# A two-layer diffusion backbone on one core: when the modulation weights are read, how their rows are turned, and how three hand-overs are made

## The chip, the cores and the metric

The kernel runs on one core of a Trainium2 chip. Its time is the time of one execution on the device in microseconds, and lower is better. A core has five engines that run their own instruction streams and wait for one another by semaphores: TensorE (PE, with its weight loads PEld), VectorE (DVE), ScalarE (ACT), GpSimd (POOL) and SyncE (SP), which here issues the loads of weights.

## The reference

Two groups of tokens, 128 of context and 256 latent ones, pass through two layers that share one set of weights. A layer is a feed-forward (SwiGLU, 1024 to 2 x 2816 and back), a token mixer, and a second feed-forward. Each of the three is `x <- LN(ALPHA*x + gate*sublayer(x*(1+scale)+shift))`, with shift, scale and gate of every channel from a conditioning vector, one for context and one for latents:

```python
mod_ctx = einsum('d,lde->le', silu(c_ctx), w_mod) + b_mod      # 9 x 1024 values per layer
mod_lat = einsum('bd,lde->lbe', silu(c), w_mod) + b_mod
x = LN(ALPHA*x + 0.5*g1*swiglu(x*(1+sc1)+sh1))
x = LN(ALPHA*x + g2*mixer(x*(1+sc2)+sh2))
x = LN(ALPHA*x + 0.5*g3*swiglu(x*(1+sc3)+sh3))
```

The mixer runs three recurrences on one input projection, each in both directions: HGRN2 and mLSTM (four heads of 128) and a Mamba-2 scan (eight heads of 64, with a short convolution); their outputs are projected, merged by sigmoid gates and projected again. In mLSTM and Mamba each pair of head and direction needs `exp(row_t - row_s)` where s comes before t and 0 elsewhere, a masked 128 x 128 matrix per block of tokens. Everything is float32. Latent scans start from given states, and the final states of the context are outputs.

## The kernel before

All 384 tokens (three blocks of 128) go through together. Activations lie with channels on partitions, `x[:, c, :]` for the eight chunks of 128 channels. Weights are read once, as units of 128 x 1024 (512 KB), in the order of use. Four buffers hold units in turn. SyncE loads one (`raw`), ScalarE rounds it to float32r (`whi`, line 974), GpSimd subtracts (`wlo`, line 519, two halves of 512 columns), and TensorE multiplies `whi*h_hi + whi*h_lo + wlo*h_hi`, three one-pass products per chunk (lines 552 to 554, or 566 to 568 where three units are taken chunk by chunk). ScalarE's program rounds unit u+3 (`ahead`) where it comes to what follows unit u, after TensorE is done with unit u-1. Splits are told by `w_split`, finished units by `w_used`.

A modulation unit is another kind: its 1024 columns are the moving operand against the four columns of the conditioning vectors (`mod_product`, line 578: four products of 512 columns a unit). Four units make a group and give 4 x 512 numbers in one bank. ScalarE copies them to `modrow`, and TensorE turns them onto partitions by four small products with `pick` (`turn`, line 585; in the prologue line 925). VectorE adds the bias (`adaln`).

The order of work on TensorE is written out by hand:
1. Prologue: the 40 units (ten groups) of the first five modulations of layer 0, in a hardware loop with one group a turn of the loop, each group turned and only then the next one begun. VectorE takes 704 of the 1024 columns of each unit's remainder here, GpSimd 320. Behind them VectorE makes the modulated input, ScalarE rounds it (`high`), VectorE subtracts (`low`), and then ScalarE rounds the first three units of the feed-forward.
2. Feed-forward: 44 gate/up units in a loop of four, two per chunk of 128 hidden channels; ScalarE's tanh and four VectorE operations make `act_hi` and `act_lo`. Then all three engines meet (`ffn_met`: each drains, raises `met` and waits for the three), and 24 down units follow, three per output chunk. At layer 1's first feed-forward the meeting also clears the semaphores.
3. Layer norm: during the down units VectorE adds the residual, centres the chunk with an early mean, and sums chunks and squares (`sx`, `sqs`; `statistics`). Behind the last chunk TensorE multiplies the sums and the last chunk by a matrix of 1/1024; VectorE subtracts the mean (`shift`), takes the reciprocal of the root, scales, and writes `h_lo` of the next input while ScalarE writes the shifted and the rounded chunk.
4. Input projection (stage "in"): eight units `hf` and four `hq` go to banks 0 and 1 in turn (the first three to 0, 1, 2), then `hi` to 2, 3, 4 and `hg` to 5, 6, 7.
5. HGRN, mLSTM, Mamba, merging, output projection. The other projections and the modulation groups (`mod`, `turn`) stand at slots between the steps of the recurrences as filling work (`mixer_order`, `HG_FILL`): 18 groups in layer 0 (all nine modulations that come next), 8 in layer 1.

In mLSTM (eight rounds) and the pair products of Mamba (sixteen) a round begins with TensorE spreading a row over all partitions (`spread`, line 773: a float32 product with one column of `ident`, which the trace shows as two passes). VectorE adds the mask (`exps`, line 1808), ScalarE takes the exponential (`pair`), VectorE multiplies by the scores (`scores`), and TensorE goes on. VectorE's program does the addition of round r+1 before the scores of round r.

## Time and profile before

| what | value |
|---|---|
| median of 3 runs | 2798.45 us (2794.81 to 2804.83) |
| the profiled execution's own time | 2796.18 us |
| its span, first to last instruction | 2794.3 us |
| TensorE busy | 2431.0 us, 87% |
| GpSimd busy | 1518.8 us, 54% |
| VectorE busy | 1196.1 us, 43% |
| ScalarE busy | 1061.3 us, 38% |
| loaded from memory | 317.35 MB |

Shares are averages over stages of different kinds: a share below 100% of the engine with the most work is either a stop or products that the clock slowed. TensorE's clock is granted at 1.0 or at 0.5 of full speed, so a stretch between the two is a mean. A line such as 552 belongs to a helper and stands for all units of its kind; windows of time tell the stages apart.

### The profile page before, as it was taken

Reading aid. Unit: us, or ns where it says so; the run is one execution under the profiler, and the core shown is the slowest. Engines: PE = TensorE matmul, PEld = TensorE weight load, DVE = VectorE, ACT = ScalarE, POOL = GpSimd, SP = SyncE. Lnnn points to the kernel's source line nnn. Section 1 sums busy time; section 2 is a strip of 40 time slices with the busy share of each in tenths; the row PEclk is TensorE's granted clock in tenths of the full one; section 3 lists DMA queues with packets and bytes.
Section 4 is the critical chain, followed back from the end, with each engine's and each line's share of the span. In section 5 each row is a group of like instructions: output and inputs, shape, how many; then the busy total and the mean of one; then the engine's idle time right before and its main releaser. Section 6 shows DMA issues by size and latency. Waiting matters only on the chain. (4 is left out here: it accounts for less than half of the span.)

```text
span 2794.3 us, 38271 instructions
## 1 busy us (share of the span) xinstructions
PE 2431.0 (87%) x13246; PEld 2222.2 (80%) x13246; DVE 1196.1 (43%) x1923; ACT 1061.3 (38%) x1631; POOL 1518.8 (54%) x1164
## 2 busy tenths in 40 slices
PE   5599989898878887799998999889987787889997
PEld 2499989787646676699998999788775676889997
DVE  4543232562565326643225331526445543663314
ACT  4333235434444443343234322452444324143322
POOL 3376545565555774466664655456743432646653
PEclk8799999999989998999999999999998888899999
DMA  8443333344343552234343333333432221324432
GB/s 277 144 141 122 118 108 109 103 129 129 102 128 94 159 158 83 83 120 123 118 128 100 124 112 118 97 113 121 144 105 83 85 66 61 98 76 135 128 111 70
DMA packets 93459, 323.16 MB, mean 116 GB/s; under 512 B 11040, under 2 KB 14368, under 8 KB 92960
## 3 DMA queue, kind: packets, MB, share of 16 engines
q1 hardware_dynamic: 87552, 312.03, 35.8%
q10 hardware_dynamic: 5792, 9.56, 1.0%
q8 instruction: 76, 1.25, 0.2%
q14 instruction: 39, 0.32, 0.0%
HBM read 317.35 MB, written 4.20 MB: 115 GB/s over the span
## 5 line engine op out<-in xcount | busy, mean ns | idle before, releaser
L519 POOL TENSOR_TENSOR wlo<-raw,whi 128x512 fp32r<-128x512 f32 (+2 forms) x1160 | 1518.6, 1335 | 1243.2 <-ACT whi L974 1182.0
L974 ACT CAST whi<-raw 128x1024 fp32r<-128x1024 f32 (+1 forms) x600 | 615.8, 1036 | 998.8 <-PE ps L554 666.4
L552 PE MATMUL ps<-h_hi,whi 128*128 128x384 f32 x2224 | 762.9, 343 | 35.2 <-DVE h_lo L2025 13.0
L554 PE MATMUL ps<-h_hi,wlo 128*128 128x384 f32 x2224 | 752.8, 339 | 0.0
L553 PE MATMUL ps<-h_lo,whi 128*128 128x384 f32 x2224 | 752.7, 338 | 0.0
L552 PEld LDWEIGHTS ps<-h_hi,whi 128*128 128x128 f32 x2224 | 425.5, 191 | 45.6 <-DVE h_lo L2025 13.6
L553 PEld LDWEIGHTS ps<-h_lo,whi 128*128 128x128 f32 x2224 | 425.4, 191 | 2.6 <-issue 2.0
L554 PEld LDWEIGHTS ps<-h_hi,wlo 128*128 128x128 f32 x2224 | 424.6, 191 | 0.0
L552 PE MATMUL ps<-act_hi,whi 128*128 128x384 f32 x704 | 241.9, 344 | 11.5 <-DVEq L458 5.9
L553 PE MATMUL ps<-act_lo,whi 128*128 128x384 f32 x704 | 240.4, 341 | 0.0
L554 PE MATMUL ps<-act_hi,wlo 128*128 128x384 f32 x704 | 240.3, 341 | 0.0
L1479 DVE SCALAR_TENSOR_TENSOR x<-ps,mod,x 128x128 f32<-128x128 f32 x96 | 35.6, 412 | 349.5 <-PE ps L554 349.5
L1560 DVE SCALAR_TENSOR_TENSOR sb<-tb,ps 128x384 f32<-128x384 f32 x88 | 48.8, 554 | 245.2 <-ACT tb L1061 245.2
L578 PE MATMUL ps<-whi,cond_s 128*4 128x512 f32 x288 | 123.7, 430 | 34.5 <-POOL wlo L519 34.5
L552 PEld LDWEIGHTS ps<-act_hi,whi 128*128 128x128 f32 x704 | 133.7, 190 | 13.3 <-DVEq L458 6.9
L1569 DVE TENSOR_TENSOR act_lo<-vb,act_hi 128x384 f32 x88 | 131.2, 1490 | 10.8
L553 PEld LDWEIGHTS ps<-act_lo,whi 128*128 128x128 f32 x704 | 133.5, 190 | 0.5
L554 PEld LDWEIGHTS ps<-act_hi,wlo 128*128 128x128 f32 x704 | 133.6, 190 | 0.0
L1563 DVE SCALAR_TENSOR_TENSOR vb<-sb,ps 128x384 f32<-128x384 f32 x88 | 48.8, 554 | 180.2 <-PE ps L554 180.0
L578 PE MATMUL ps<-wlo,cond_s 128*4 128x512 f32 x288 | 121.2, 421 | 0.0
L686 PE MATMUL ps<-q,kk 128*128 128x128 f32 x768 | 98.3, 288 | 22.8 <-DVEq L458 14.0
L686 PEld LDWEIGHTS ps<-q,kk 128*128 128x128 f32 x768 | 95.0, 202 | 28.0 <-DVEq L458 14.8
(311 smaller groups left out, 3011.7 us busy)
## 6 DMA issues: line engine op xcount, KB each, us to landing
raw<-in_w_in SPq DMA_DIRECT2D x248, 512.0 KB, 3.5
raw<-in_w_gu SPq DMA_DIRECT2D x176, 512.0 KB, 3.4
raw<-in_w_down SPq DMA_DIRECT2D x64, 512.0 KB, 3.4
raw<-in_w_mod SPq DMA_DIRECT2D x40, 512.0 KB, 4.5
raw<-in_w_down SPq DMA_DIRECT2D x32, 384.0 KB, 3.0
raw<-in_w_branch SPq DMA_DIRECT2D x24, 512.0 KB, 3.4
raw<-in_w_out SPq DMA_DIRECT2D x16, 512.0 KB, 3.4
x<-in_x ACTq DMA_DIRECT2D x1, 1536.0 KB, 6.9
```

Of the source, the lines that this page charges most:

```text
L519: last = nc.gpsimd.tensor_tensor(wlo[s][:, a:b], raw[s][:, a:b], whi[s][:, a:b].bitcast(F32), ALU.subtract)
L552: mm(out, hi_, xh[:, xc, :], start=start and n == 0, stop=False)
L553: mm(out, hi_, xl[:, xc, :], start=False, stop=False)
L554: last = mm(out, lo_, xh[:, xc, :], start=False, stop=stop and n == len(chunks) - 1)
L578: last = mm(bank[0:4, :], cond_s[:, 2 * m + c, :], w[s][:, c * MIX:(c + 1) * MIX], start=(m == 0 and c == 0 and w is whi), stop=(m == 3 an ...
L686: last = mm(out, kk[:, d, g, cols], (q if what == "diag" else qd[d])[:, g, cols], start=True, stop=True)
L974: act.copy(whi[m][:, 0:w], raw[m][:, 0:w]).then_inc(w_hi, 1)
L1479: last = stt(x[:, b, a:c], ps[b % 2][:, a:c], mod[:, col, gi:gi + 1], x[:, b, a:c], ALU.mult, ALU.add)
L1560: step(stt(sbf[jj][:, :], tb[jj][:, :], 1.0, ps[2 * jj][:, 0:T], ALU.add, ALU.mult))
L1563: stt(vb[jj][:, :], sbf[jj][:, :], 0.5, ps[2 * jj + 1][:, 0:T], ALU.mult, ALU.mult).then_inc(gated, 1)
L1569: step(tt(act_lo[:, bass.ds(f, 1), :], vb[jj][:, :].unsqueeze(1), act_hi[:, bass.ds(f, 1), :].bitcast(F32), ALU.subtract))
```

## The change

Sixteen of the 40 modulation units stay in the prologue (shift and scale of the first feed-forward); the other 24 stand between the gate/up units of layer 0's first feed-forward, whose loop is written out on TensorE and ScalarE. In the prologue a group no longer waits for the turning of the group before. Rows of up to four groups lie on partitions 0, 32, 64 and 96 of `modrow` and are turned together. The meetings between gate/up and down go: TensorE waits for the last pair's product, and in its first down block for the remainders third by third (`ff_lo`); the clearing in layer 1 stays. In layer norm the sums cover six chunks in place of seven, and shifting and scaling alternate from the third chunk on; a Tanh table load stands right behind the norm. The first projections of the mixer use banks 0 to 4 in turn. The mask is added by TensorE in one accumulation with the row, which is split in two float32r parts, and ScalarE's exponential reads the bank. The constants `ident` and `neg` are cast to float32r at the start.

The core of the diff, with names and lists cut where they only follow:

```diff
+U_PRO = 2 * KC
+U_FIRST = U_MOD0 - U_PRO
...
+GROUPS_OF = [MOD_GROUPS] * (L - 1) + [2 * (U_MOD - U_MOD0) // KC]
+BATCH = 4
+def first_order():
+    order, mods, turns, pairs = [("gu", k) for k in range(4)], 0, [], NF - 4
+    for n in range(2, NF):
+        order += [("gu", 2 * n), ("gu", 2 * n + 1)]
+        order += [("turn", b) for b in turns]
+        turns = []
+        while mods < min(U_FIRST, (n - 1) * U_FIRST // pairs):
+            order.append(("mod", mods))
+            mods += 1
+            if mods % (4 * BATCH) == 0 or mods == U_FIRST:
+                turns.append(1 + (mods - 1) // (4 * BATCH))
...
+FIRST = first_order()
+GU_AT = {k: a for kind, k, a in FIRST if kind == "gu"}
...
+                if n % 2 == 0:
+                    out += one("mod", g)
+                elif g % BATCH == BATCH - 1 or g == groups - 1:
+                    out += one("turn", g // BATCH)
...
-    hg = (one("gr", 0, 1) + one("mod", 0) + one("mv", 0) + one("turn", 0) + one("mv", 1, 2) + one("mod", 1)
-          + one("mv", 3) + one("turn", 1) + one("mq", 0, 1) + one("mod", 2) + one("mq", 2) + one("turn", 2)
-          + one("mq", 3) + one("mod", 3) + one("mk", 0) + one("turn", 3) + one("mk", 1) + one("mod", 4)
-          + one("mk", 2) + one("turn", 4) + one("mod", 5) + one("mk", 3) + one("turn", 5))
+    hg = (one("gr", 0, 1) + one("mod", 0) + one("mv", 0, 1, 2) + one("mod", 1) + one("mv", 3) + one("mq", 0, 1)
+          + one("mod", 2) + one("mq", 2, 3) + one("mod", 3) + one("mk", 0) + one("turn", 0) + one("mk", 1)
+          + one("mod", 4) + one("mk", 2) + one("mod", 5) + one("mk", 3))
...
-                    kind, banks = "tm", (2, 3, 4) if name == "hi" else (5, 6, 7)
+                    kind, banks = "tm", (2, 3, 4) if name == "hg" else (5, 6, 7)
                 else:
                     kind = name if name in ("mod", "turn") else "fm"
-                    pool = {"rows": (3, 4), "ml": (3, 3), "pairs": (3, 7)}.get(stage, (0, 1))
-                    banks = (b if name == "hf" and b < LEAD else pool[k % 2],)
+                    pool = {"in": (0, 1, 2, 3, 4), "rows": (3, 4), "ml": (3, 3), "pairs": (3, 7)}.get(stage, (0, 1))
+                    banks = (pool[k % len(pool)],)
...
-                pe.wait_ge(ln_y, j + 1)
-                mm(ps[5][:, 0:T], mean_w[:, :], sx[:, :], start=True, stop=False)
-                pe.wait_ge(ln_q, (KC - 1) * (j + 1))
-                mm(ps[6][:, 0:T], mean_w[:, :], sqs[:, :], start=True, stop=False)
-                pe.wait_ge(ln_cent, KC * (j + 1))
-                mm(ps[5][:, 0:T], mean_w[:, :], x[:, KC - 1, :], start=False, stop=True).then_inc(ln_mean, 1)
-                pe.wait_ge(ln_sq, KC * (j + 1))
-                mm(ps[6][:, 0:T], mean_w[:, :], sq[(KC - 1) % 4][:, :], start=False, stop=True).then_inc(ln_acc, 1)
+                for n in range(-1, 2):
+                    if n < 0:
+                        pe.wait_ge(ln_y, j + 1)
+                    else:
+                        pe.wait_ge(ln_cent, KC * j + KC - 1 + n)
+                    last = mm(ps[5][:, 0:T], mean_w[:, :], sx[:, :] if n < 0 else x[:, KC - 2 + n, :], start=(n < 0),
+                              stop=(n == 1))
+                    if n == 1:
+                        last.then_inc(ln_mean, 1)
+                    if n < 0:
+                        pe.wait_ge(ln_q, SUMMED * (j + 1))
+                    else:
+                        pe.wait_ge(ln_sq, KC * j + KC - 1 + n)
+                    last = mm(ps[6][:, 0:T], mean_w[:, :], sqs[:, :] if n < 0 else sq[(KC - 2 + n) % 4][:, :],
+                              start=(n < 0), stop=(n == 1))
+                last.then_inc(ln_acc, 1)
+            def first_units():
+                for kind, k, u in FIRST[4:]:
+                    if kind == "turn":
+                        pe.wait_ge(rows0_out, (U_PRO + min(16 * k, U_FIRST)) // 4)
+                        turn(ps[4 + k]).then_inc(turned0, 1)
+                        continue
+                    unit_split(pe, 0, u)
+                    if kind == "gu":
+                        if k % 2 == 0:
+                            pe.wait_ge(gated, k // 2 + 1)
+                        block_product(ps[k % 4][:, 0:T], u, h_hi, h_lo, [(c, c) for c in range(KC)], True,
+                                      True).then_inc(w_used, 1)
+                        continue
+                    if k and k % 4 == 0:
+                        pe.wait_ge(rows0_out, (U_PRO + k) // 4)
+                    mod_product(ps[7], u, k % 4).then_inc(w_used, 1)
...
-                ffn_met(pe, l, j, "pe")
+                if l == j == 0:
+                    first_units()
...
+                counts_reset(pe, l, j, "pe")
...
+                pe.wait_ge(gated, at + NF + 2)
                 for b in range(KC):
                     pe.wait_ge(resid, 2 * KC * j + b + 1)
                     for third in range(KTHIRDS):
-                        u = u0 + U_GU + KTHIRDS * b + third
+                        u = down_at(l, j, u0) + KTHIRDS * b + third
                         unit_split(pe, l, u)
+                        if b == 0:
+                            pe.wait_ge(ff_lo, at + 2 + min(KC * (third + 1), NF))
...
-            def spread(r, rr):
+            def spread(r, d, rr):
+                out = ps[r % 2][:, 0:T]
                 if r >= 2:
-                    pe.wait_ge(pr_x, r - 1)
-                mm(ps[r % 2][:, 0:T], ident[:, rr:rr + 1].to_broadcast([P, P]), x_5[:, :], start=True,
-                   stop=True).then_inc(pr_bc, 1)
+                    pe.wait_ge(pr_e, r - 1)
+                mm(out.rearrange("p (a b) -> p a b", b=P), ident_r[:, :], neg[:, d:d + 1, :].to_broadcast([P, NT, P]),
+                   start=True, stop=False)
+                row = ident_r[:, rr:rr + 1].to_broadcast([P, P])
+                mm(out, row, x_5h[:, :], start=False, stop=False)
+                mm(out, row, x_5l[:, :], start=False, stop=True).then_inc(pr_bc, 1)
...
-            with pe.Fori(0, U_MOD0 // 4) as i:
+            for i in range(U_PRO // 4):
+                if i >= 2:
+                    pe.wait_ge(rows0_out, i - 1)
                 for m in range(4):
                     pe.wait_ge(w_split, i * 4 + (m + 1 + NRAW))
-                    mod_product(ps[0], m, m).then_inc(w_used, 1)
-                pe.wait_ge(rows0_out, i + 1)
...
+                    mod_product(ps[i % 2], m, m).then_inc(w_used, 1)
+            pe.wait_ge(rows0_out, U_PRO // 4)
+            turn(ps[7]).then_inc(turned0, 1)
...
+            def mod_rows(g, bank):
+                return act.copy(modrow[32 * (g % BATCH):32 * (g % BATCH) + 4, :], bank[0:4, :])
+            for i in range(U_PRO // 4):
+                for m in range(4):
+                    k = i * 4 + m + AHEAD
+                    if k == U_PRO + 1:
+                        break
+                    ahead(0, k - AHEAD - U_PRO) if k == U_PRO else round_unit(k // 4, k % 4)
                 act.wait_ge(w_used, i * 4 + (4 + NSPLIT))
-                act.wait_ge(turned0, i + 1)
...
+                mod_rows(i, ps[i % 2]).then_inc(rows0_out, 1)
+            for k in range(1, AHEAD):
+                ahead(0, k - AHEAD)
...
-                for n in range(KC + 1):
+                shifted(j + 1, 0)
+                rounded(j + 1, 0)
+                for n in range(1, KC + 1):
                     if n < KC:
                         shifted(j + 1, n)
-                    if n:
+                    if n > 1:
                         rounded(j + 1, n - 1)
+            def first_units():
+                for kind, k, u in FIRST:
+                    if kind == "turn":
+                        continue
+                    ahead(0, u)
+                    if kind == "gu" and k % 2:
+                        unit_done(act, 0, GU_AT[k - 1])
+                        act.wait_ge(gated, k // 2 + 1)
+                        af(tb[k // 2 % 2][:, :], ps[(k - 1) % 4][:, 0:T], ACT.Tanh, scale=0.5).then_inc(gate_t, 1)
+                    elif kind == "mod" and k % 4 == 3:
+                        g = (U_PRO + k) // 4
+                        unit_done(act, 0, u)
+                        act.wait_ge(turned0, g // BATCH)
+                        mod_rows(g, ps[7]).then_inc(rows0_out, 1)
...
-                act.wait_ge(pr_x, r + 1)
+                act.wait_ge(pr_bc, r + 1)
                 if r >= 2:
                     act.wait_ge(pr_s, r - 1)
                     if r <= 9:
                         act.wait_ge(ml_kw, min(r - 1, 8))
...
-                    last = af(pr[r % 2][:, c], pt[r % 2][:, c], ACT.Exp, bias=t_1[:, t, rr:rr + 1])
+                    last = af(pr[r % 2][:, c], ps[r % 2][:, c], ACT.Exp, bias=t_1[:, t, rr:rr + 1])
...
+                af(eps[:, 2:3], eps[:, 0:1], ACT.Tanh)
...
-                shift(2)
-                shift(3)
...
+                def normalised(n):
+                    dve.wait_ge(ln_sub, KC * j + n + 1)
+                    tt(x[:, n, :], x[:, n, :], rstd[:, :], ALU.mult).then_inc(ln_out, 1)
+                normalised(0)
+                normalised(1)
+                for n in range(2, KC + 2):
                     if n < KC:
...
+                        shift(n)
+                        normalised(n)
+                    if not final:
...
+                def pair(i, jj, up):
+                    dve.wait_ge(gate_t, i * 2 + (at + jj + 1))
+                    step(stt(sbf[jj][:, :], tb[jj][:, :], 1.0, ps[2 * jj][:, 0:T], ALU.add, ALU.mult))
+                    unit_done(dve, l, up)
+                    step.done()
+                    dve.wait_ge(ff_lo, i * 2 + (at + jj + 1))
+                    stt(vb[jj][:, :], sbf[jj][:, :], 0.5, ps[2 * jj + 1][:, 0:T], ALU.mult,
+                        ALU.mult).then_inc(gated, 1)
+                    dve.wait_ge(gated, i * 2 + (at + jj + 3))
+                    f = bass.ds(i * 2 + jj, 1)
+                    step(cp(act_hi[:, f, :], vb[jj][:, :].unsqueeze(1)))
+                    step.done()
+                    tt(act_lo[:, f, :], vb[jj][:, :].unsqueeze(1), act_hi[:, f, :].bitcast(F32),
+                       ALU.subtract).then_inc(ff_lo, 1)
+                if l == j == 0:
+                    def done(ins_):
+                        step(ins_)
...
-                ffn_met(dve, l, j, "dve")
+                    for n in range(NF):
+                        pair(n // 2, n % 2, GU_AT[2 * n + 1])
+                    dve.wait_ge(turned0, 2)
+                    adaln((2, 3), turned_groups(ps[5], 4), bmod0[:, U_PRO:U_PRO + 16], done)
+                    dve.wait_ge(turned0, 3)
+                    adaln((4,), turned_groups(ps[6], 2), bmod0[:, U_PRO + 16:U_MOD0], done)
...
+                step(cp(x_5h[:, :], x_5[:, :]))
+                step.done()
+                step(tt(x_5l[:, :], x_5[:, :], x_5h[:, :].bitcast(F32), ALU.subtract))
...
-            def exps(r, d):
-                dve.wait_ge(pr_bc, r + 1)
-                if r >= 2:
-                    dve.wait_ge(pr_e, r - 1)
-                tt(pt[r % 2][:, :].rearrange("p (a b) -> p a b", b=P),
-                   neg[:, d:d + 1, :].to_broadcast([P, NT, P]),
-                   ps[r % 2][:, 0:T].rearrange("p (a b) -> p a b", b=P), ALU.add).then_inc(pr_x, 1)
...
+            cp(hmask[:, :, :, :], hmask_in[:, :, :, :])
+            cp(ident_r[:, :], ident_in[:, :])
+            cp(neg[:, :, :], neg_in[:, :, :])
```

## Rows read from the trace of the kernel before

**Rows 1.** Stretches: us, busy PE, PEld, DVE, ACT, POOL (count), clock, DMA, GB/s.

```profile
121.92:307.14 185.22, 185.22 (x1056) 184.90 (x1056) 65.59 (x85) 53.38 (x65) 117.32 (x88) 0.99 0.40 124
940.60:1052.20 111.60, 100.07 (x546) 80.98 (x545) 30.27 (x75) 55.79 (x101) 84.36 (x66) 0.98 0.50 156
2101.00:2154.60 53.60, 40.32 (x200) 28.76 (x198) 36.85 (x104) 20.71 (x50) 20.03 (x16) 0.87 0.34 98
309.11:313.90 4.79, 4.79 (x18) 4.79 (x19) 0.00 (x0) 1.03 (x1) 2.52 (x2) 0.64 0.01 2
436.70:440.20 3.50, 3.50 (x13) 3.50 (x12) 3.50 (x3) 1.58 (x3) 3.50 (x3) 0.51 0.34 105
```

**Rows 2.** Timeline of the start: start, duration, engine, line, operation [idle before].

```profile
26.82 0.57 ACT L1000 COPY modrow<-ps 4x512 f32<-4x512 f32 x1
...
85.33 0.40 PE L578 MATMUL ps<-whi,cond_s 128*4 128x512 f32 x1
...
85.57 0.40 PE L578 MATMUL ps<-wlo,cond_s 128*4 128x512 f32 x1
...
94.64 2.28 DVE L1415 TENSOR_TENSOR x<-x,pos 128x2048 f32<-128x2048 f32 x1
...
100.37 0.57 ACT L1000 COPY modrow<-ps 4x512 f32<-4x512 f32 x1 [6.84 <-PE ps L578]
...
104.79 0.56 DVE L1460 TENSOR_TENSOR h_lo<-ht,h_hi 128x384 fp32r<-128x384 f32 x1
...
112.36 3.88 ACT L974 CAST whi<-raw 128x1024 fp32r<-128x1024 f32 x4
...
121.92 0.66 PE L566 MATMUL ps<-h_hi,whi 128*128 128x384 f32 x1 [19.79 <-POOL wlo L519]
```

**Rows 3.** Timeline of TensorE in the first HGRN stage.

```profile
543.93 1.05 PE L585 MATMUL ps<-pick,modrow 4*128 4x2 f32 x8
547.36 2.05 PE L686 MATMUL ps<-q,kk 128*128 128x128 f32 x8 [2.38 <-DVE att L1681]
```

**Rows 4.** Timeline of GpSimd in gate/up; line 1569's group (busy, mean ns).

```profile
144.76 8.30 POOL L519 TENSOR_TENSOR wlo<-raw,whi 128x512 fp32r<-128x512 f32 x6
154.38 2.54 POOL L519 TENSOR_TENSOR wlo<-raw,whi 128x512 fp32r<-128x512 f32 x2 [1.31 <-ACT whi L974]
...
L1569 DVE TENSOR_TENSOR act_lo<-vb,act_hi 128x384 f32 x88 | 131.2, 1490 | 10.8
```

**Rows 5.** Timeline around the last hand-over from gate/up to down.

```profile
2676.62 0.56 DVE L1563 SCALAR_TENSOR_TENSOR vb<-sb,ps 128x384 f32<-128x384 f32 x1 [2.39 <-PE ps L554]
...
2677.82 0.56 DVE L1569 TENSOR_TENSOR act_lo<-vb,act_hi 128x384 f32 x1
...
2678.48 0.44 PE L552 MATMUL ps<-act_hi,whi 128*128 128x384 f32 x1 [1.98 <-DVEq L458]
```

**Rows 6.** Timeline of the first layer norm.

```profile
404.66 0.81 PE L598 MATMUL ps<-sx,mean_w 128*128 128x384 f32 x2
...
405.30 0.81 PE L600 MATMUL ps<-sqs,mean_w 128*128 128x384 f32 x2
...
406.25 0.91 PE L602 MATMUL ps<-x,mean_w 128*128 128x384 f32 x2
...
412.80 0.56 DVE L1543 TENSOR_TENSOR x<-x,rstd 128x384 f32<-128x384 f32 x1
...
416.53 0.55 DVE L1460 TENSOR_TENSOR h_lo<-ht,h_hi 128x384 fp32r<-128x384 f32 x1
...
417.23 0.66 PE L566 MATMUL ps<-h_hi,whi 128*128 128x384 f32 x1 [9.42 <-DVE h_lo L1460]
```

**Rows 7.** Timeline of TensorE in the first input projection.

```profile
435.69 0.44 PE L552 MATMUL ps<-h_hi,whi 128*128 128x384 f32 x1 [3.03 <-ACT kk L1303]
```

**Rows 8.** Timeline of VectorE in mLSTM and of TensorE in layer 1's pair products.

```profile
760.64 0.55 DVE L1808 TENSOR_TENSOR pt<-neg,ps 128x384 f32<-128x384 f32 x1
...
2296.69 0.88 PE L880 MATMUL ps<-xt,st 128*128 128x64 f32 x6 [1.25 <-DVE st L1823]
```

311 lines of the change are left out of this document (151 added, 160 removed).

## The prediction

> **What bounds the kernel now.** I read the stage table first (one line per stretch, busy time of each engine and granted clock), then the timeline at each place where TensorE stands still. In the first feed-forward TensorE is busy for all of the 185.2 us of its gate/up stretch and GpSimd for 117.3; in the pair products of layer 0's Mamba part TensorE has 100 of 112 us [rows 1]. So the end is set by TensorE: by its products, by the stretches in which it has nothing to multiply, and by those at half clock behind such a stop. Time is to be had in four places: the start, where it waits for modulations; breaks at hand-overs; small products in its own queue; and the mLSTM rounds, where in layer 1 it has 40 of 54 us and VectorE 37 [rows 1].
>
> **The start.** Now 40 modulation units run ahead of the feed-forward in ten groups, and the copies of their rows are at 26.82 and 100.37 us, so a group takes 73.55 / 9 = 8.17 us. Behind the last group ScalarE rounds eight chunks of the input, and only then the first weights of the feed-forward (112.36 us); GpSimd has to split them, and TensorE starts at 121.92 [rows 2]. With four groups, and no turning behind each, a group takes about 8.17 less one turning of 1.05 [rows 3], 7.1 us; the position add of 2.28 us [rows 2] comes between, of which I charge 1. The fourth copy (0.57) then starts at 26.8 + 3 x 7.1 + 1 = 49.1 and ends at 49.7. The first weight unit is rounded ahead of that copy, the other two behind it, at 1 us each (four took 3.88 [rows 2]). GpSimd needs 2.5 us for a unit [rows 4]; the second unit can begin at 50.7, so the third is split at 55.8. The other path (turning, four small operations less two, first chunk) ends before that by the spacing of the same steps now: 4.98 us from the last copy to the first remainder would give 54 or 55 (the last copy at 100.37, that remainder's end at 105.35 [rows 2]). TensorE starts at 56 instead of 121.9: **-66 us**, between -60 (8.17 us for each group and all of the add) and -74 (a group as short as ScalarE's four casts and a copy, 4.5).
>
> **The moved units.** 24 units with four products of 512 columns each come into the gate/up loop, spaced 0.24 us at full clock as now [rows 2]: 24 x 4 x 0.235 = 22.5 us; two turnings cost 2.1. They lengthen the stretch only by that if the four weight buffers stay full. Per two gate/up units (8.3 us: 185.2 x 2 / 44, with the slow start in it, less 0.1) come 1.33 modulation units, 1.25 us, so TensorE uses 3.33 units in 9.6 us. GpSimd splits a free unit in 2.54 us [rows 4]: 8.5 us, and VectorE's two copies per pair take from it what the longer halves show (six in 8.30 where free ones would take 7.6 [rows 4], at two pairs 0.35 each) and at most their own 0.36 + 0.56: 8.8 to 9.4 us. That fits, narrowly, and the schedule has at most two modulation units in a row behind two long ones. ScalarE has 3.33 casts of 1, a tanh and a third of a row copy, under 5 us of 9.6. SyncE issues the same loads in another order. VectorE's eight chunk multiplications and three constant casts now all stand ahead of its first pair, which is due four units, 17 us, after TensorE starts; I cost them at nothing (8 x 0.55 [rows 8] and three of at most 2.28 make 11 us, and that is what they cost uncovered). **+24.6 us**, at most +44 (below).
>
> The Trainium skill, page "SBUF — State Buffer", section "SBUF: two separate sides", speaks against this part: VectorE and GpSimd share a pair of SBUF ports as an exclusive lock, held for the whole instruction, and a VectorE operation with two SBUF inputs waits for a GpSimd one and the other way round. The trace bears it out: the remainder of the activations takes 1490 ns on average, and 560 when GpSimd stands still [rows 4, 5]. Since every modulation unit is more GpSimd work at the side of the same VectorE work, the rule makes GpSimd the engine that could take over; it is the first rival below.
>
> **Hand-over from gate/up to down.** In three of the four feed-forwards a meeting of three engines goes and two direct waits stand in its place. Now TensorE stops for 1.98 us and VectorE's last product of the pair needs 0.56 of it [rows 5]; the rest is the copy, the remainder's issue and the meeting. The new wait is on that product, behind it in TensorE's queue are the first two thirds of the down block, which need only early chunks; the last remainder is due 8 us later. Stop 0.75 instead of 1.98: 3 x 1.2 = 3.7. Behind the stop the clock was 0.64 over 4.79 us and 18 products ran in place of 27, 1.6 us lost [rows 1]; this I saw behind two of the three, and take half of it. **-5.3**, between -2 and -7. The fourth keeps its reset.
>
> **Layer norm.** One sum fewer on each side: TensorE gets x6 and its square as two more products of 0.64 us in front of x7, and in the feed-forward norms its queue is already the later one: the products of the sums start at 404.66 and 405.30, that of x7 at 406.25 [rows 6]; it would start at 407.25, +1.0. The reciprocal no longer waits for two shifts, which now outlast ScalarE's root by an estimated 0.5, and behind it four operations instead of eight stand before the first remainder (412.80 to 416.53 is eight, 0.47 each): -1.9, of which ScalarE's rounding lets 1.75 through. TensorE's break of 9.42 us [rows 6] gets shorter by 1.25. At the two norms behind the output projection VectorE's sums are late, so the two moved sums help where they cost above: an estimate of 2.25 + 0.25 each. The last norm has no remainder and loses the 1.0 and a shift, 1.4 in all; the one ahead of layer 1 loses 0.9, since its fourth weight waits for the end of VectorE's work, which two shifts (0.94) move back. 2 x 1.25 + 2 x 2.5 - 1.4 - 0.9: **-5**, between -9 and +2.
>
> **Input projection.** Behind the leading products TensorE waits 3.03 us for a bank that ScalarE has to empty [rows 7]; with five banks in turn it doesn't, and next waits about 0.6 for the split of the following unit, whose cast still comes behind the first bank's two copies. Behind the stop the clock was 0.51 for 3.5 us, some 1.7 us lost [rows 1]. 2 x (2.4 + 1.7): **-8**, or -3 if the new wait keeps the clock down. The early table load stands where ScalarE idles.
>
> **Turnings and masks in the mixers.** 26 turnings become 7, each 1.0 us of TensorE [rows 3]. The first three of each HGRN stage stand ahead of a wait for VectorE (2.38 us behind the first [rows 3]), so they give nothing. Three in layer 0's mLSTM give nothing either: there the modulation groups 6 and 7 now stand in rounds 0 and 1 instead of 0 and 2, eight units in two rounds, where GpSimd needs 8 x 2.54 = 20 us; I charge what VectorE gains there against it. That leaves about 9: **-9**. The mask: VectorE's addition, 0.55 us a round [rows 8], goes; TensorE makes three one-pass products (185.2 / 1056 = 0.175 each [rows 1], 0.53) where a two-pass one takes 0.64, as the sums' products of the same shape [rows 6]. No row shows such a product of the identity; between the 128x384 one-pass spacing and three times the two-pass price (1.9) I take the first, since its operands have that type and shape. In layer 1's mLSTM VectorE's chain sets the rounds: 8 x 0.55: **-4.5**. In the pair products 32 x 0.11 = 3.5, and in rounds without filling work, where TensorE waits 1.25 us [rows 8], about 0.6 in five of them: **-6.5**. The two casts added to the row stage stand ahead of a long wait for ScalarE. Ends for these three: 0 (other waits close up) and -35 (every turning, all 48 additions, clock drops).
>
> **Sum.** -66 + 24.6 - 5.3 - 5 - 8 - 9 - 4.5 - 6.5 = -79.7. The profiled execution took 2796.2 us, 2.3 below the median of three; 2796.2 - 79.7 = **2716 us**.
>
> **Rivals.**
> GpSimd sets the gate/up loop (the rule above, at its worst). If every half takes the 1.6 us that the two blocked ones of those six need (8.30 less four free ones), a unit takes 3.2 and 3.33 units 10.7 us against 9.6: 18 pairs x 1.1 = 20 us, and 2736. For: 9.4 of 9.6 us at the upper bound. Against: two of six halves are blocked now, and the number of VectorE operations stays. 15%.
> The hand-overs, turnings and masks give nothing, since the next wait is as late: 33 us (-5.3 - 8 - 20) come back, 2749. For: the 2.38 us behind a turning; against: most sit in stretches where TensorE is over 90% busy. 15%.
> Fewer stops keep the clock up, and all that was halved counts: 2690. 12%.
> Slower than before: a modulation unit is split only when TensorE comes to it. Then each costs a cast of 1.0 and a split of 2.54, 3.6 us x 24 = 86, and half clock behind each of 18 breaks, 1.6 x 18 = 29: 2716 + 115 = 2831. It decides from 80 / 24 = 3.3 us per unit. For: where four such units follow each other the buffers do run dry; against: three units are prepared ahead and long ones stand between. 3%.
> My forecast has 55%, with 2702 to 2730 as its own range.
>
> **Range and chances.** 2694 to 2747 takes in the second and third rival's middle. What this kernel's measurement can tell from no change is 0.3%, 8 us: faster by more than that 0.96, within it 0.01, slower 0.03.
>
> **What would show it.** Right: the first leading product near 56 us; the gate/up stretch near 210 us with TensorE busy throughout; stops of 0.7 us at the down blocks; no stop behind the leading products of the projection. Wrong: waits of modulation products for GpSimd inside the loop; a break ahead of x7's product longer than now without an earlier first remainder; in layer 0's mLSTM a stop of over 6 us in round 1.

## The result, and the profile after

The changed kernel takes 2714.07 us, the median of four runs (2711.78 to 2715.61); the kernel before took 2796.63 us in the same session. The ratio is 0.9704, with a 95% interval of 0.9687 to 0.9721, so the change takes off 3%, 82.6 us. The prediction was 2716. The profiled execution took 2712.65 us, with a span of 2710.8.

The same three stretches as in [rows 1] come first: the first gate/up stretch, layer 1's mLSTM and layer 0's pair products. The columns are length, busy time and count of TensorE, its weight loads, VectorE, ScalarE and GpSimd, then granted clock, DMA share and GB/s.

```profile
56.27:265.84 209.57, 209.53 (x1168) 195.56 (x1168) 70.87 (x119) 83.91 (x102) 176.96 (x136) 0.99 0.56 170
2031.40:2081.40 50.00, 36.14 (x200) 28.63 (x200) 32.42 (x96) 20.50 (x50) 19.99 (x16) 0.86 0.38 105
884.30:988.30 104.00, 94.43 (x537) 79.99 (x536) 24.25 (x59) 53.76 (x98) 86.99 (x68) 0.98 0.56 172
```

The gate/up stretch is 24.4 us longer (185.22 before) and still has no hole in TensorE, though GpSimd's work went from 117 to 177 us. The other two windows, whose ends are set by eye, are shorter by 3.6 and 7.6 us; from first to last product of the stage (the first row product to the last with `cs`, the first weighted product to the last), layer 1's mLSTM is 4.8 us shorter and layer 0's pair products 7.0.

The start, as in [rows 2] (start, duration, engine, line, operation, idle before):

```profile
48.43 0.57 ACT L1077 COPY modrow<-ps 4x512 f32<-4x512 f32 x1 [0.66 <-PE ps L619]
49.06 1.06 PE L626 MATMUL ps<-pick,modrow 128*128 128x8 f32 x8 [0.66 <-ACT modrow L1077]
50.57 4.98 POOL L561 TENSOR_TENSOR wlo<-raw,whi 128x512 fp32r<-128x512 f32 x4 [0.23 <-ACT whi L1052]
55.62 0.54 DVE L1555 TENSOR_TENSOR h_lo<-ht,h_hi 128x384 fp32r<-128x384 f32 x1
56.31 0.66 PE L607 MATMUL ps<-h_hi,whi 128*128 128x384 f32 x1 [6.20 <-DVE h_lo L1555]
```

GpSimd ends the third unit's split at 55.55 us and VectorE the first remainder at 56.16: the two paths that I had worked out (55.8 and 54 to 55) end within 0.6 us of each other, and TensorE starts at 56.31 instead of 121.92.

The hand-over to the down blocks, as in [rows 5], then the last product of the means and the first leading product behind the first norm, as in [rows 6]:

```profile
266.52 0.44 PE L593 MATMUL ps<-act_hi,whi 128*128 128x384 f32 x1 [0.65 <-DVE vb L1662]
...
363.12 0.81 PE L643 MATMUL ps<-x,mean_w 128*128 128x384 f32 x2
...
371.81 0.66 PE L607 MATMUL ps<-h_hi,whi 128*128 128x384 f32 x1 [7.24 <-DVE h_lo L1555]
```

The group of the activations' remainders, as in [rows 4] (count, then busy time, mean ns of one, idle before):

```profile
L1668 DVE TENSOR_TENSOR act_lo<-vb,act_hi 128x384 f32 (+1 forms) x88 | 118.2, 1343 | 8.9
```

The stop at the first down block is 0.65 us where it was 1.98 (as at the last one in [rows 5]), the break of the norm 7.24 where it was 9.42, and a remainder 1343 ns on average where it was 1490. One loss is much larger than forecast, ahead of layer 1's fourth weight unit. First the kernel before, then the changed one, each from the first leading product of layer 1 on:

```profile
1479.61 0.66 PE L566 MATMUL ps<-h_hi,whi 128*128 128x384 f32 x1 [9.43 <-DVE h_lo L1460]
...
1487.09 3.21 DVE L1550 TENSOR_SCALAR x<-x,lnal 128x384 f32<-128x384 f32 x8
...
1490.94 1.28 ACT L974 ACT_TABLE_LOAD   x1 [4.42 <-DVE x L1550]
...
1495.94 0.45 PE L552 MATMUL ps<-h_hi,whi 128*128 128x384 f32 x1 [1.29 <-POOL wlo L519]
```

```profile
1411.74 0.66 PE L607 MATMUL ps<-h_hi,whi 128*128 128x384 f32 x1 [7.23 <-DVE h_lo L1555]
...
1423.77 1.25 DVE L1649 TENSOR_SCALAR x<-x,lnal 128x384 f32<-128x384 f32 x3
...
1425.68 1.28 ACT L1052 ACT_TABLE_LOAD   x1 [4.42 <-DVE x L1649]
...
1426.97 1.99 ACT L1052 CAST whi<-raw 128x1024 fp32r<-128x1024 f32 x2
1428.09 3.74 POOL L561 TENSOR_TENSOR wlo<-raw,whi 128x512 fp32r<-128x512 f32 x3 [26.90 <-ACT whi L1052]
...
1430.64 0.69 PE L593 MATMUL ps<-h_hi,whi 128*128 128x384 f32 x1 [4.39 <-POOL wlo L561]
```

ScalarE waits for VectorE's last operation of the norm, loads a table, casts, GpSimd splits, and TensorE has stood still for 4.39 us (1.29 before). The queue is the same in both kernels, down to ScalarE's wait of 4.42 us and the load of 1.28. Counted from where TensorE falls idle ahead of its leading product (1470.18 and 1404.51), VectorE's last operation ends 20.1 us later before and 20.5 now, only 0.4 more; but the leading products start 2.2 us earlier in that count, so what the norm's break won comes back as a stop at the fourth unit.

By TensorE's own events the 83.5 us between the two profiled executions divide so: start -65.6; first gate/up with its stop +23.0; down block and norm behind it -2.8; input projections -4.7 and -4.2; layer 0's mixer with the norm behind it -15.0, layer 1's -15.5; layer 0's second feed-forward -1.4 and its norm -1.3; layer 1's first gate/up +5.3, the norm behind it -1.1; the last feed-forward -0.5, the last norm +0.4.

### The profile page after: what moved, and what is told of

Read it like the earlier page. It is cut to its first block, busy times and chain, and to the rows that moved or that the text cites. A ratio compares the mean times of both kernels' runs of the same rounds, so it can differ in the third digit from the quotient of the medians.

```text
span 2710.8 us, 37419 instructions
## 1 busy us (share of the span) xinstructions
PE 2385.8 (88%) x13110; PEld 2201.3 (81%) x13110; DVE 1152.6 (43%) x1848; ACT 1057.0 (39%) x1614; POOL 1560.9 (58%) x1188
## 4 chain that ended last, share of the span: by engine, by line
issue 45%; POOL 44%; PE 10%; POOLq 1%; DVE 1%; ACT 0%; DVEq 0%
POOL wlo L561 44%; PE ps L593 3%; PE ps L595 3%; PE ps L594 3%; POOLq L573 0%; POOLq L575 0%; DVE x L1637 0%; DVE x L1622 0%; DVE x L1649 0%; DVE rstd L1631 0%; PE ps L643 0%; PE ps L651 0%; PE ps L634 0%; ACT std L1125 0%; DVE vb L1662 0%
## 5 line engine op out<-in xcount | busy, mean ns | idle before, releaser
L561 POOL TENSOR_TENSOR wlo<-raw,whi 128x512 fp32r<-128x512 f32 (+2 forms) x1184 | 1560.7, 1345 | 1115.7 <-ACT whi L1052 1085.7
L593 PEld LDWEIGHTS ps<-h_hi,whi 128*128 128x128 f32 x2224 | 424.0, 191 | 45.5 <-DVE h_lo L2132 13.6
L1668 DVE TENSOR_TENSOR act_lo<-vb,act_hi 128x384 f32 (+1 forms) x88 | 118.2, 1343 | 8.9
```

The lines of the kernel that those rows point to most:

```text
L561: last = nc.gpsimd.tensor_tensor(wlo[s][:, a:b], raw[s][:, a:b], whi[s][:, a:b].bitcast(F32), ALU.subtract)
L593: mm(out, hi_, xh[:, xc, :], start=start and n == 0, stop=False)
L1668: tt(act_lo[:, f, :], vb[jj][:, :].unsqueeze(1), act_hi[:, f, :].bitcast(F32), ALU.subtract).then_inc(ff_lo, 1)
```

## The experiments

Times are medians of at least five executions, each beside the kernel before on the same chip; ratios are to that, and differences are to 2714.07 us of the changed kernel unless the text says otherwise. The kernel before took 2794.6 to 2796.9 us in these sessions, so a difference of 2 us between sessions says nothing. Lengths of stages are taken from TensorE's events in the profiled execution, of which there is one for each kernel.

**The order of ScalarE's queue alone (on the kernel before).**

```diff
             round_unit(U_MOD0 // 4 - 1, AHEAD)
+            ahead(0, -AHEAD)
             rows_out(U_MOD0 // 4 - 1)
+            for k in range(1, AHEAD):
+                ahead(0, k - AHEAD)
...
-                if l == j == 0:
-                    for k in range(AHEAD):
-                        ahead(l, k - AHEAD)
```

> The kernel before, with all 40 modulation units still ahead of the feed-forward; only the casts of the first three feed-forward units stand where the change puts them: one ahead of the last row copy, two right behind it, all ahead of the eight roundings of the input. Theory (part of the start's gain is the order of ScalarE's queue, not the number of units): the three splits of 2.54 us run from about 98.5 us, beside the last products and the turning, and end near 107; TensorE's first leading product comes at 107 to 109 instead of 121.9, 13 to 15 us of the 65.6 that the start gave, and the whole kernel takes 2782 us (2780 to 2786). Rival (the start waits for the chunks of the input, and GpSimd's splits only happen to end with them): the first product stays above 118, and the kernel takes 2793 to 2797.

Measured: 2781.74 us, ratio 0.995 (0.9936 to 0.9965). The end of the start, in the timeline of that kernel:

```profile
98.57 0.57 ACT L1000 COPY modrow<-ps 4x512 f32<-4x512 f32 x1 [2.62 <-PE ps L578]
99.05 1.99 ACT L974 CAST whi<-raw 128x1024 fp32r<-128x1024 f32 x2
107.41 0.66 PE L566 MATMUL ps<-h_hi,whi 128*128 128x384 f32 x1 [6.26 <-DVE h_lo L1460]
```

TensorE starts at 107.41, as the theory has it, and what it waits for last is now VectorE's first remainder. Of the start's 65.6 us, 14.5 came from three casts that no longer stand behind eight roundings; they could have been had without moving one modulation unit.

**Modulation units in fours.**

```diff
-        while mods < min(U_FIRST, (n - 1) * U_FIRST // pairs):
+        while mods < min(U_FIRST, (n - 1) * U_FIRST // pairs // 4 * 4):
```

> The changed kernel, with the 24 modulation units of the first gate/up loop in six groups of four, where the change sets one or two of them between two pairs of gate/up units; the same units and products, another order of the loads. Theory (the loop stayed TensorE's because three units are prepared ahead and at most two short ones stand in a row; GpSimd is just behind): four short units take TensorE 3.8 us while GpSimd needs 2.54 to 2.9 us for each unit, so behind every group TensorE waits 0.7 to 2.5 us for GpSimd, with some 1.6 us lost at half clock where the stop is long enough: 6 x (0.7 to 4.1) = 4 to 25 us, 2718 to 2739, with waits for GpSimd's remainder in the loop. Rival (GpSimd is well ahead, and the order within the loop is of no matter): 2712 to 2716, and no such wait.

Measured: 2738.5 us, ratio 0.9788 (0.9767 to 0.9809), 24 us longer. TensorE's waits in the loop, of the kernel with fours (engine, tile, line, releaser: total, times, longest):

```profile
PE ps L593 <- POOL wlo L561: 8.3, 6, 1.4
PE ps L619 <- POOL wlo L561: 7.4, 6, 1.3
```

The changed kernel has no such line in its loop. The waits make 15.7 us, and 13.6 us at 1.2 GHz behind three of the six groups another 6.8. So GpSimd was near the edge, as the first rival said, and the order of the units is what kept the loop TensorE's.

**The mask back on VectorE, and the mask back with the cheaper products.** Both take the mask's product out of TensorE and add it on VectorE; the second keeps the row product in two one-pass halves.

```diff
-                mm(out.rearrange(...), ident_r[:, :], neg[:, d:d + 1, :].to_broadcast([P, NT, P]), ...)
-                mm(out, row, x_5h[:, :], start=False, stop=False)
-                mm(out, row, x_5l[:, :], start=False, stop=True).then_inc(pr_bc, 1)
+                mm(out, ident[:, rr:rr + 1].to_broadcast([P, P]), x_5[:, :], start=True, stop=True).then_inc(pr_bc, 1)
...
+                tt(pt[r % 2]..., neg[:, d:d + 1, :]..., ps[r % 2]..., ALU.add).then_inc(pr_x, 1)
```

> The changed kernel, with the mask added by VectorE again (48 additions) and one two-pass product a round in place of three one-pass ones. Theory (the mask is worth more than I predicted, since the rounds of the pair products are VectorE's chain and not TensorE's): layer 1's pair products get longer by 4.8 us, layer 0's by 5 to 8, layer 1's mLSTM by 4.5 to 5, layer 0's by 0 to 3: 2714 + 15 to 20 = 2729 to 2734. The sizes as predicted (0.11 us a round of TensorE and a few rounds of 0.6, and 4.5 in layer 1's mLSTM): 2725. Rival (those stages gained from fewer turnings, and the mask only moved the work): within 3 us of 2714.

> The changed kernel, with the mask added by VectorE again (48 additions of about 0.55 us), while TensorE's row product stays in two one-pass products (0.35 us a round, where the changed kernel has 0.53 and the kernel with the whole mask back 0.64 or more). It splits the 23 us that putting the mask back cost between the two engines. Theory (VectorE's addition stands in the chain from TensorE's row product to ScalarE's exponential, and that is what was under-priced): most of the 23 us stay, 2730 to 2738. Rival (the passes of TensorE's product, dearer at half clock, are the cost): 48 x 0.18 = 9 us less than the changed kernel at best, 2705 to 2718.

Measured: 2737.24 us, ratio 0.9784 (0.9766 to 0.9803), and 2734.22 us, ratio 0.9784 (0.9763 to 0.9804). Layer 1's pair products, from the first weighted product to the last: first the changed kernel, then the mask back, then the mask back with one-pass halves (columns as in the first table).

```profile
2200.38:2274.12 73.74, 71.36 (x432) 70.28 (x432) 15.74 (x50) 30.21 (x69) 31.48 (x24) 0.97 0.26 79
```

```profile
2220.19:2298.82 78.63, 75.12 (x418) 70.23 (x418) 24.02 (x65) 31.79 (x69) 30.31 (x24) 0.95 0.23 74
```

```profile
2215.62:2292.38 76.76, 72.66 (x417) 71.58 (x418) 23.87 (x65) 31.79 (x69) 30.41 (x24) 0.92 0.25 76
```

Of the 23 us, 20 stay when TensorE's product is cheap: most of the cost comes with VectorE's addition, as the theory of the second run says. Not all of it is the addition's own: in both runs layer 1's HGRN stage, which has no mask, is 2.9 us longer, with 15.6 us at 1.2 GHz under its products in place of 9.0. In rounds without filling work TensorE stops for 0.69 to 1.01 us in the changed kernel, and the clock stays up behind all three stops; with the addition in the chain the stops are 0.82 to 1.54 us, and behind some of them follow 3.4 us at 1.2 GHz. The shortest rounds, those without filling work, are 2.04 us against 2.73. The rival of the first run, that turnings had made the gain, falls: layer 1 has none in its pair products, and with the whole mask back they take 87.1 us to the transposition behind them, as in the kernel before, where the changed kernel takes 82.2.

**Turnings one by one.**

```diff
-                elif g % BATCH == BATCH - 1 or g == groups - 1:
-                    out += one("turn", g // BATCH)
+                out += one("turn" if n % 2 else "mod", mod[n // 2])
...
-                    turn(ps[banks[0]]).then_inc(turned, 1)
+                    turn_one(ps[banks[0]]).then_inc(turned, 1)
```

> The changed kernel, with the modulation groups inside both mixers turned one by one, in the order and slots of the kernel before (19 turnings more; the start and the first feed-forward stay as changed). Theory (a turning costs TensorE its 1 us only where it isn't ahead of a wait): layer 0's HGRN stage gets longer by 3, its pair products by 3, layer 1's HGRN by 0; layer 0's mLSTM loses 4 turnings' gain but has its modulation units in rounds 0, 2, 4 and 6 again and gets shorter or stays (-3 to +1): 2714 + 3 to 7 = 2717 to 2721. As predicted (9 us): 2723. Rival (turnings always stand ahead of another wait): 2711 to 2716.

Measured: 2722.22 us, ratio 0.9733 (0.9715 to 0.9751): 8.2 us, just above the theory's range and close to the predicted 9. Layer 0's HGRN stage gets 2.6 us longer, its state stage 1.4, its pair products 3.6, and layer 1's mixer 3.4, 2.2 of it in HGRN, where the theory had 0; layer 0's mLSTM gets 0.6 shorter.

**Seven-chunk sums again.**

```diff
-        SHIFT_N, SUMMED = 3, KC - 2
+        SHIFT_N, SUMMED = 3, KC - 1
```

> The changed kernel, with VectorE summing seven chunks and seven squares again in all norms; the new order behind the reciprocal stays. Theory as predicted (the moved sums cost TensorE 1.0 us at the norms behind the feed-forwards and save 2 to 2.25 at the two behind the output projection): the breaks of 7.24 us at layers' first and last norms shrink to 6.2 to 6.5, the two middle norms get 2 us longer; net -1 to +1, 2712 to 2716. Rival (the shorter sums are what shortened all norms, the order behind the reciprocal little): every norm gets 1 to 2 us longer, 2719 to 2726.

Measured: 2709.36 us, ratio 0.9695 (0.9674 to 0.9716), outside both ranges; its interval overlaps the changed kernel's, and the spans of the profiles are 1.7 us apart. The stages say more than the time: the breaks stay at 7.23 us in all norms, so the order behind the reciprocal alone made them shorter; the rival falls on that, and so do the theory's 6.2 to 6.5 us. The moved sums cost 0.9 us at each norm behind a feed-forward and save 0.3 and 0.4 at the two middle ones, not 2 to 2.25.

**Layer 1's fourth cast early.**

```diff
                 if l:
+                    ahead(l, UF1)
                     act.wait_ge(ln_x, KC * 4)
...
+                    if not j:
+                        gu(0, u0, False)
-                    with act.Fori(0, U_GU // 4 - 1) as i:
+                    with act.Fori(0 if j else 1, U_GU // 4 - 1) as i:
```

> The changed kernel, with one cast moved: at the head of layer 1, ScalarE casts the fourth weight unit ahead of its wait for VectorE's last eight operations of the norm and of the load of the new parameters, not behind them. Theory (the 5.3 us that layer 1's first gate/up stretch got longer are the stop of 4.4 us for that unit's split and the half clock behind it): the stop falls under 1 us, the 6.8 us at half clock behind it go, and the kernel takes 2706 to 2709, with the distance from the first leading product of layer 1 to its first down product 193 to 186 us instead of 193. Rival (the loop's next unit or the first tanh is as late, and the stop moves on): 2712 to 2716.

Measured: 2707.31 us, ratio 0.9692 (0.9671 to 0.9713). TensorE's waits at the head of layer 1, of the changed kernel and of this one:

```profile
PE ps L607 <- DVE h_lo L1555: 7.2, 1, 7.2
PE ps L593 <- POOL wlo L561: 4.4, 1, 4.4
```

```profile
PE ps L607 <- DVE h_lo L1559: 7.2, 1, 7.2
PE ps L593 <- DVE vb L1666: 1.1, 1, 1.1
```

The wait for GpSimd is gone, 1.1 us for VectorE's product is next, and the distance from the leading product to the down block is 192.3 us, where it was 198.0 in the changed kernel and 192.8 before (the 193 of the theory's last words is the kernel before's). The times' intervals overlap; the stage alone shows the cause.

**Layer 0's modulation groups spread over the mLSTM rounds.**

```diff
-            + spread("ml", 8, gated(mod=(6, 7, 8, 9)))
+            + ([("ml", s, *it) for s, it in zip((0, 2, 3, 4, 6), gated(mod=(6, 7, 8, 9)))] if l == 0 else
+               spread("ml", 8, gated(mod=(6, 7, 8, 9))))
```

> The changed kernel, with layer 0's modulation groups 6 to 9 in rounds 0, 2, 4 and 6 of the mLSTM as before, not in 0, 1, 4 and 6 (their turning stays joined, in round 3). Theory (eight units in two rounds are more than GpSimd can split in that time, and TensorE's waits for it, 1.4 us twice, and the half clock behind them cost what VectorE's lighter chain gained there): layer 0's mLSTM, 79 us, gets 3 to 5 us shorter, the kernel takes 2709 to 2712. Rival (the rounds without filling work wait for VectorE anyway, and one round more or less of cover changes nothing): 2713 to 2716.

Measured: 2715.44 us, ratio 0.9712 (0.9691 to 0.9733). TensorE's largest waits in that stage, of the changed kernel and of this one:

```profile
PE ps L866 <- DVE cs L1959: 13.1, 4, 5.0
PE ps L619 <- POOL wlo L561: 3.5, 3, 1.4
```

```profile
PE ps L867 <- DVE cs L1960: 14.6, 4, 4.8
```

The waits for GpSimd go and VectorE's get longer; the stage is 83.3 us from its first row product to the transposition of its output, against 84.2. My theory falls: VectorE's chain sets these rounds.

**Two banks again in the input projection.**

```diff
-                    pool = {"in": (0, 1, 2, 3, 4), "rows": (3, 4), "ml": (3, 3), "pairs": (3, 7)}.get(stage, (0, 1))
-                    banks = (pool[k % len(pool)],)
+                    pool = {"rows": (3, 4), "ml": (3, 3), "pairs": (3, 7)}.get(stage, (0, 1))
+                    banks = (b if name == "hf" and b < LEAD else pool[k % 2],)
```

> The changed kernel, with two banks in turn for the input projection behind its leading products, as before, in place of five. Theory as predicted (a stop of 3.0 us for a bank and half clock behind it, 4.1 us a layer): a stop of about 3 us for ScalarE's copy comes back behind the leading products of both layers, and the distance from the first leading product of the projection to the HGRN stage (92.7 us in both layers of the changed kernel) gets 4 to 4.5 us longer: 2722 to 2723. Rival (the early load of the tanh table, which stays, is what shortened it): within 2 us of 2714.

Measured: 2713.63 us, ratio 0.971 (0.9692 to 0.9728): no difference. The stop behind the leading products, the answer to [rows 7], in this kernel:

```profile
388.60 0.44 PE L593 MATMUL ps<-h_hi,whi 128*128 128x384 f32 x1 [1.62 <-ACT kk L1405]
```

So the banks took 1.62 of the 3.03 us, and the rest of the change 1.41 and the half clock behind the stop. That rest is the table load: in the kernel before it stands between ScalarE's first two reads of the projection, in this one it is over before them, at 382.42 us (rows of ScalarE, before and with two banks).

```profile
431.64 0.49 ACT L1302 ACTIVATE ff<-ps 128x384 f32<-128x384 f32 x1 [6.55 <-PE ps L568]
432.14 1.28 ACT L1303 ACT_TABLE_LOAD   x1
433.44 0.49 ACT L1303 ACTIVATE kk<-ps 128x384 f32<-128x384 f32 x1
```

```profile
385.97 0.49 ACT L1404 ACTIVATE ff<-ps 128x384 f32<-128x384 f32 x1 [2.38 <-PE ps L609]
386.36 0.49 ACT L1405 ACTIVATE kk<-ps 128x384 f32<-128x384 f32 x1
```

From the start of the first read to the end of the second it is 2.29 us in the one and 0.88 in the other. The projection is 1.7 us longer with two banks (1.9 in layer 1), and layer 0's HGRN stage 2.2 us shorter. The windows from the projection's end on show where that comes from, of the changed kernel and of this one:

```profile
457.48:459.90 2.42, 0.00 (x0) 0.00 (x0) 0.00 (x0) 2.42 (x7) 0.00 (x0) 1.00 0.55 168
459.90:470.10 10.20, 5.63 (x26) 5.63 (x27) 5.32 (x7) 4.79 (x9) 3.06 (x2) 0.50 0.07 18
470.10:480.00 9.90, 9.90 (x67) 9.90 (x66) 4.95 (x5) 1.43 (x2) 2.53 (x2) 1.00 0.22 56
```

```profile
459.00:462.70 3.70, 0.00 (x0) 0.00 (x0) 0.00 (x0) 3.70 (x10) 0.00 (x0) 1.00 0.44 142
462.70:469.50 6.80, 3.51 (x16) 3.51 (x17) 4.53 (x5) 3.51 (x7) 2.41 (x2) 0.50 0.01 2
469.50:480.00 10.50, 10.50 (x74) 10.50 (x73) 5.27 (x6) 1.43 (x2) 3.17 (x3) 1.00 0.18 51
```

Both kernels stop for 6.99 us ahead of the HGRN stage. In the changed one the clock falls 2.4 us into the stop and stays down for 10.2 us, and again for 3.4 us 33 us into the stage; in the other it falls 3.7 us into the stop, for 6.8 us, and not again. Under HGRN's products that makes 9.1 us at 1.2 GHz against 3.5. What the banks saved was given back there; that they are what moved the clock isn't shown.

**An earlier wait at the down blocks.**

```diff
-                pe.wait_ge(gated, at + NF + 2)
+                pe.wait_ge(gated, at + NF + 1)
```

> The changed kernel, with TensorE's wait ahead of the down block set to the last but one pair's product (the one that leaves free the two banks that the down block writes) in place of the last pair's. Theory (the 0.65 to 0.8 us that are left of the hand-over are that wait alone; the first two thirds need only chunks made long before): three stops go, 2 to 2.5 us in all, and the fourth, with the counters' reset in it, stays at 5.8: 2711 to 2712 in time, 2708.5 in the profiled span of 2710.8. Rival (the next weight unit's split, or the remainder that the first third waits for, is as late): stops of 0.5 us or more stay at the down blocks, 2713 to 2715.

Measured: 2705.52 us, ratio 0.9681 (0.966 to 0.9701). The three stops (0.65, 0.81 and 0.80 us) are gone. From the 24th product ahead of each to the 72nd behind it, the three places are 0.9, 1.1 and 1.1 us shorter, 3.1 in all. The span is 4.1 us shorter rather than 2.3, and here too both HGRN stages begin with 6.8 us at 1.2 GHz instead of 10.2, although layer 0's stop lies at the same place in the span as in the changed kernel, from 457.48 to 464.47 us:

```profile
457.48:461.25 3.77, 0.00 (x0) 0.00 (x0) 0.00 (x0) 3.77 (x10) 0.00 (x0) 1.00 0.43 139
461.25:468.07 6.82, 3.60 (x17) 3.60 (x18) 4.53 (x5) 3.44 (x6) 2.50 (x2) 0.50 0.01 2
```

So 3.1 of the 8.5 us between the medians are at the wait; how the rest divides between the clock and the spread of single executions (2702.78 to 2711.51 us for this kernel) stays open.

**What the runs point to, joined**: the early cast, the earlier wait, and six-chunk sums in the middle norms alone.

```diff
-        SHIFT_N, SUMMED = 3, KC - 2
+        SHIFT_N, SUMMED = 3, (KC - 1, KC - 2, KC - 1)
+        Q_BASE = [sum(SUMMED[:j]) for j in range(4)]
```

> The changed kernel with what the runs point to joined: the fourth weight unit of layer 1 cast ahead of the wait for the norm's last operations (6.4 us in the spans of the profiles), seven-chunk sums again in the norms behind the feed-forwards and six-chunk sums only in the two behind the output projection (four times about 0.9 to 1.1 us), and the earlier wait at the down blocks (2 to 2.5 us). Theory (the three are at different places and add up): 2714 - 6.4 - 4 - 2 = 2702, range 2700 to 2705. Rival (they shift the same later waits): no better than the cast alone, 2706 to 2708.

Measured: 2704.64 us, ratio 0.9672 (0.9654 to 0.9691), inside the theory's range. The span is 13.2 us shorter than the changed kernel's, although layer 1's row and mLSTM stages, whose code is the same, came out 3 us longer (126.5 against 123.4).

**TensorE kept busy ahead of the HGRN stage**, on the joined version:

```diff
+                pe.wait_ge(evac, evac_of[l]["hq", 3])
+                for _ in range(30):
+                    mm(ps[0][:, 0:T], ident_r[:, :], h_hi[:, 0, :], start=True, stop=True)
                 meet(pe, MEET["hg_in", 0])
```

> The joined version, with 30 products of the identity with a chunk of the input (128x384, one pass, 0.175 us each, 5.2 us; nobody reads what they write) on TensorE in each of the two stops of 6.99 us ahead of the HGRN stage. The stop's end is set by ScalarE's copies of the projection, so they delay nothing. In the joined version TensorE's granted clock falls to its lower level 3.9 us into that stop and stays there for 6.8 us, the last 3.8 of them under HGRN's products. Theory (what TensorE does in the stop decides the clock, and HGRN's first products lose 1.9 us by it): no stretch at the lower level there, the HGRN stage gets 1.5 to 2 us shorter in each layer, 2704.6 - 3 to 4 = 2701 (2699 to 2703). Rival (the clock falls all the same, or VectorE, which follows those products, takes as long): within 1.5 us of 2704.6.

Measured: 2699.1 us, ratio 0.9659 (0.9645 to 0.9672). The stop and the first of layer 0's HGRN:

```profile
455.40:462.40 7.00, 5.22 (x31) 4.90 (x30) 2.08 (x3) 6.19 (x15) 0.00 (x0) 1.00 0.28 77
462.40:472.00 9.60, 9.60 (x73) 9.60 (x73) 5.00 (x6) 2.45 (x3) 4.03 (x3) 1.00 0.17 55
```

The clock stays at 2.4 GHz throughout these two windows, so the first half of the theory holds in layer 0 (in layer 1, 3.4 us at 1.2 GHz still followed). The second half doesn't: the HGRN stage is 163.1 us against 163.2. What follows its next stop, for VectorE, shows why: there the clock falls for 3.4 us in this kernel and not at all in the joined one (first this kernel, then the joined one).

```profile
494.07:497.49 3.42, 3.42 (x19) 3.42 (x18) 0.24 (x1) 0.00 (x0) 3.20 (x3) 0.50 0.42 120
```

```profile
494.00:498.00 4.00, 3.32 (x27) 3.26 (x28) 2.14 (x4) 0.00 (x0) 4.00 (x4) 1.00 0.42 134
```

Under the stage's products that makes 3.4 us at 1.2 GHz against 3.7: the half clock moved and hardly shrank. The time came out as the theory had it, but the 3.4 us between the spans lie in layer 1's later stages (123.7 against 126.5 us in its rows and mLSTM), which the edit doesn't touch. So this is the fastest version that ran, below the changed kernel by more than both intervals, but that the idle products are what made it faster than the joined one isn't shown.

## Why the prediction was right, step by step

The time was 2716 against 2714.07, and its mechanism held: TensorE's stream sets the end, 66 us come from the start and some 24 go back into the loop. Inside the sum several terms were wrong in size, with opposite signs, and that so little is left is in part luck: the mixers without their norms gained 4.5 us more than their three terms and the hand-overs 1.4 more, while layer 1's fourth unit lost 3 more. The range doesn't take in what its text says: the middles of the second and third rival, 2749 and 2690, lie just outside 2694 to 2747.

- **Start**: -66 predicted, -65.6 measured, and by the two paths named. What I hadn't priced apart is that 14.5 of it belong to the order of ScalarE's queue.
- **Moved units**: +24.6 predicted, +24.4 for the stretch. No modulation product waited for GpSimd. The exclusive port that the Trainium skill states (page "SBUF — State Buffer", section "SBUF: two separate sides") agrees with the remainder's 1343 ns on average beside 0.56 us when GpSimd stands still. But GpSimd kept pace; with four short units in a row it didn't, and then a unit cost 1 us more on average, not the 3.3 from which the slower rival would have decided.
- **Hand-over**: -5.3 predicted. The stops went from 1.98 to 0.65, 0.81 and 0.80, which is the 3.7 of the sum. The half clock that stood behind two of the three went too, and I had counted half of it: from the 24th product ahead of each stop to the 72nd behind it the three places gained 2.9, 1.2 and 2.7, together 6.7. One line moved took another 3.1.
- **Layer norm**: -5 predicted, about -4 measured. The order behind the reciprocal gave 2.2 us at every norm, where the working has 0.5 and 1.75, and the sums cost 0.9 behind the feed-forwards (1.0). The two middle norms gained 2.1 and 4.0 us where I had 2.5 each; under their products 0.9 us more at 1.2 GHz than before in the first and 3.2 less in the second account for the difference. The moved sums' part of that is 0.3 and 0.4, so of "2.25 + 0.25" the 2.25 fits only as the order's; the theory of the run with seven-chunk sums took it for the sums'. The term for the norm ahead of layer 1 was mis-sized: 0.9 lost in all, where the norm gained 1.3 and the stretch behind it lost 5.3. I gave the loss to VectorE's tail, which moved back by 0.4; but the chain of the fourth unit (wait, table load of 1.28 us, cast, split) kept its length while the leading products came 2.2 us earlier, and with the longer stop came 6.8 us at 1.2 GHz, where there were none. The early cast gave 5.8 us of that stage back.
- **Input projection**: -8 predicted, -8.9 measured from leading product to HGRN. The step's cause failed: I gave nearly all of the 3.03 us to the banks and nothing to the table load; without the banks 1.41 of it went, and all of the half clock behind it. The banks made the projections 1.7 and 1.9 us shorter, and in the profiled executions 5.5 us more at half clock in layer 0's HGRN stage outweighed layer 0's part of that.
- **Turnings**: -9 predicted, 8.2 by undoing.
- **Masks**: -11 predicted (4.5 and 6.5), 23 by undoing. Of the 26 us between those two profiled spans, 6.6 lie in the pair products (1.7 in layer 0, 4.9 in layer 1), as predicted; 4.2 and 7.0 in the mLSTM stages, where I had 0 and 4.5; and 3.3 in the HGRN stages, which have no mask. The term that was too small is VectorE's addition in mLSTM, but 23 is more than the change gained by it: with the mask back the mLSTM stages are 2.6 us longer than in the kernel before in both layers, and the mixers as a whole gained 24.5 without their norms, where undoing masks and turnings one at a time makes 31. From before to after, the mLSTM stages gained 1.5 and 4.4. The modulation groups stand closer together there now; in layer 1 that isn't the reason for the 2.6, since with the mask back and one-pass halves, in the same order, the stage is 0.5 us shorter than before. Which part is the clock isn't shown: layer 1's mLSTM stage took 70.7 to 73.6 us in kernels with the same code for it.
- **Sum**: -79.7 against -83.5 between the profiled executions.

## What to carry to other kernels

When a break gets shorter, follow the other chains that start in it (here wait, table load, cast, split) to the engine that sets the end: one that keeps its length becomes the next stop, and a stop of 4.4 us in place of 1.3 cost the clock as well. An operation between two engines in a chain counts in the rounds that have no filling work (2.73 us with the addition, 2.04 without), so count the rounds by their filling and not by the busy shares. Before moving work, look whether the order of one queue hides part of the gain. And where a run undoes one step to price it, compare its stages with the kernel before too: undoing can cost more than the step gained.

## What the runs showed of the hardware

In every kernel but the one with idle products TensorE stops for 7.0 us ahead of each HGRN stage, and its clock falls to 1.2 GHz within that stop. In the 13 profiled stops in which it fell 2.1 to 2.9 us after the start, it stayed down for 10.2 us; in the 13 in which it fell 3.4 to 4.2 us after the start, for 6.8. With the changed mixers the long stretch was each time followed by another 3.4 us or more at the stage's next long stop, and the short one never. In these kernels, the one with single turnings aside, layer 0's HGRN stage took 163.1 to 163.2 us behind the short stretch (five kernels, the one with idle products among them) and 165.4 to 165.8 behind the long one (six kernels). So a stage that an edit doesn't touch can add or take 2 us. Whether the edit or the single execution decides it isn't shown, as one execution of each kernel was profiled; the place in the span doesn't, as the changed kernel and the one with the earlier wait show, whose stops lie at the same microseconds. The Trainium skill (page "TensorE: Matmul & The Clock Gate", section "What's actually happening") says that the activity window behind the clock is free-running and doesn't reset when the kernel starts; the stretches of those two kernels agree with that.
